# Issuing 29 small GpSimd loads of the front in quarter 3 instead of quarter 2, on one core

## The reference

```
sh1, sc1, gt1, sh2, sc2, gt2 = split(silu(c) @ w_ada + b_ada, 6)     # 9 conditioning rows, w_ada 2048 x 12288
h = rmsnorm(x, g_mix) * (1 + sc1) + sh1
qa, ka, va, qb, kb, vb, rb, ab = split(h @ w_in)                      # w_in 2048 x 4368
lg = log_sigmoid(ab @ w_gla_gate + b_gla_gate) / 16
oa = attention over a window, with learned sinks
     (prompt: own keys; sample: cache_swa_k, cache_swa_v and the new keys)
s_new, ob = gated linear attention(state_gla, qb, kb, vb, lg)
x = x + gt1 * (concat(oa, rmsnorm_head(ob, g_gla_norm) * silu(rb)) @ w_out)
h = rmsnorm(x, g_ffn) * (1 + sc2) + sh2
x = x + gt2 * top-2 of 32 experts(h)                                  # 3 x 4 MB of weights each, all 32 are read
y = rmsnorm(x, g_final)
```

## Time and profile before

| | |
|---|---|
| time, median of 3 runs | 1881.46 us (1879.25 to 1883.17) |
| the profiled execution: its own time | 1879.52 us |
| its span in the trace | 1877.9 us |
| TensorE busy | 1572.9 us, 84% |
| VectorE, ScalarE, GpSimd busy | 400.1, 201.2, 180.5 us |
| weights and large tensors, queue q1 | 562.29 MB, 73.8% of the engines' time |
| GpSimd's queue q0 | 41.68 MB, 7.3% |

### The profile page before, as it was taken

One profiled execution on the slowest core, in us unless ns is written; L12 is line 12 of the kernel. 1 busy time (PEld: TensorE's weight loads), 2 busy tenths in 40 slices (PEclk: granted clock), 3 DMA queues, 4 the chain that ended last, 5 costly groups with the idle time before them and its releaser, 6 DMA issues.

```text
span 1877.9 us, 21572 instructions
## 1 busy us (share of the span) xinstructions
PE 1572.9 (84%) x8837; PEld 812.9 (43%) x8837; DVE 400.1 (21%) x882; ACT 201.2 (11%) x505; POOL 180.5 (10%) x369
## 2 busy tenths in 40 slices
PE   6899999999999999958879888787877778888740
PEld 2355454444454444545445444444444344444320
DVE  2012222224232310452111111111111111111115
ACT  3001111111211100110000000000000000000003
POOL 1301000000101020030101001010101010101002
PEclk9999999999999999969889899999999998989985
DMA  9987777666623583199999999999999999999962
GB/s 365 336 291 289 280 280 290 245 257 230 224 68 101 179 247 118 68 332 397 426 426 427 427 427 428 426 423 426 427 426 424 425 421 420 417 426 426 426 246 96
DMA packets 101700, 610.94 MB, mean 325 GB/s; under 512 B 15950, under 2 KB 18110, under 8 KB 65418
## 3 DMA queue, kind: packets, MB, share of 16 engines
q1 hardware_dynamic: 84242, 562.29, 73.8%
q0 software_dynamic: 16592, 41.68, 7.3%
q10 hardware_dynamic: 816, 6.29, 0.8%
HBM read 603.03 MB, written 28.40 MB: 336 GB/s over the span
## 4 chain that ended last, share of the span: by engine, by line
PE 49%; DMA 43%; DVE 3%; issue 1%; ACT 1%; POOL 1%; SPq 0%; POOLq 0%; DVEq 0%; ACTq 0%
DMA ring<-in_w_expert_up 36%; PE bank L811 9%; PE bank L1111 7%; PE bank L807 7%; PE bank L1239 7%; DMA zbuf<-h_rows,cur 4%; PE bank L1260 3%; PE bank L765 3%; PE bank L1138 2%; PE bank L752 2%; DMA ring<-in_w_ada 2%; PE bank L731 1%; PE bank L756 1%; DMA ring<-in_w_in 1%; DVE ring L2122 1%
## 5 line engine op out<-in xcount | busy, mean ns | idle before, releaser
L1239 PE MATMUL bank<-ring,zbuf 128*64 128x256 f32 x4096 | 462.6, 382 | 81.0 <-DMA ring<-in_w_expert_up 72.7
L1239 PEld LDWEIGHTS bank<-ring,zbuf 128*64 128x64 f32 x4096 | 291.8, 137 | 259.7 <-DMA ring<-in_w_expert_up 94.9
L1260 PE MATMUL bank<-ring,hbuf 128*64 128x512 f32 x1024 | 270.5, 689 | 17.7 <-ACT hbuf L1550 17.7
L811 PE MATMUL bank<-ring,hbuf 128*128 128x512 f32 x384 | 174.2, 599 | 2.9 <-ACT xbuf L1343 2.6
L1260 PEld LDWEIGHTS bank<-ring,hbuf 128*64 128x64 f32 x1024 | 82.8, 158 | 185.7 <-issue 184.2
L807 PE MATMUL bank<-hbuf,ring 128*128 128x384 f32 x384 | 133.8, 495 | 1.2 <-ACT zbuf L1339 0.8
L1111 PE MATMUL bank<-ring,zbuf 128*128 128x512 f32 x288 | 128.7, 602 | 3.1 <-DVE ring L1858 1.9
L2027 DVE TENSOR_SCALAR hbuf<-hbuf 128x256 f32<-128x256 f32 x32 | 9.4, 294 | 520.2 <-ACT hbuf L1542 520.2
L811 PEld LDWEIGHTS bank<-ring,hbuf 128*128 128x128 f32 x384 | 70.2, 190 | 83.7 <-issue 82.7
L807 PEld LDWEIGHTS bank<-hbuf,ring 128*128 128x128 f32 x384 | 69.7, 190 | 52.5 <-issue 11.0
L631 POOL CAST cur<-stab 128x1 int32 (+1 forms) x32 | 5.7, 178 | 861.1 <-DVE zbuf L2035 861.1
(11 more groups left out here) (381 smaller groups left out, 1148.4 us busy)
## 6 DMA issues: line engine op xcount, KB each, us to landing
ring<-in_w_expert_gate SPq DMA_DIRECT2D x64, 2048.0 KB, 25.0
ring<-in_w_expert_down SPq DMA_DIRECT2D x64, 2048.0 KB, 23.3
ring<-in_w_expert_up SPq DMA_DIRECT2D x64, 2048.0 KB
ring<-in_w_ada SPq DMA_DIRECT2D x96, 1024.0 KB, 8.2
ring<-in_w_in SPq DMA_DIRECT2D x32, 1024.0 KB, 9.0
ring<-in_w_out SPq DMA_DIRECT2D x16, 1024.0 KB, 5.1
ring<-y_rows ACTq DMA_DIRECT2D x3, 2048.0 KB, 12.4
xbuf<-in_x_prompt SPq DMA_DIRECT2D x4, 1024.0 KB, 5.8
```

The lines of the kernel that those rows point to most:

```text
L811: last = mm(bank[t][:, :], hT[:, k, t * P:(t + 1) * P], w[:, kk_, :], start=(k == 0), stop=(k == KC - 1))
L1239: last = mm(bank[2 + u][64 * q:64 * q + 64, 256 * (j // 4):256 * (j // 4) + 256], xeT[u][:, k % 8, k // 8, :], w[:, kk_, 256 * q:256 * q + ...
L1260: last = mm(bank[5 + n][64 * q:64 * q + 64, :], hidT[u][:, k % 2, k // 2, :], unit(8 + k)[:, 1024 * q + QN * n:1024 * q + QN * n + QN], st ...
```

## The change

The wait of GpSimd at line 501 is raised from `modT_ps` 4 to 7, so that the 29 transfers are issued behind `columns(3, 0)` in place of `columns(1, 1)`. The order among them changes as well: the sinks, the gate's weight and bias and the head gain now come ahead of the second norm's gain and the bias rows. The transfers are the same 29 with the same sizes, and nothing else is changed.

```diff
-            pool.wait_ge(modT_ps, 4)
+            pool.wait_ge(modT_ps, 7)
             ck = A["cache_swa_k"][0].rearrange("b w j c -> w b j c")
             for u in range(2):
                 for j in range(SWA_KV):
                     g.dma_start(cache_k2[:, :, j, u, :], ck[:, :, j, :]).then_inc(cache_in, 16)
             g.dma_start(cache_v[:, :, :], A["cache_swa_v"][0].rearrange("b w j c -> w b (j c)")).then_inc(cache_in, 16)
+            pool.wait_ge(gate_zero, 1)
+            g.dma_start(sinkb[:, :], A["attn_sinks"].broadcast_to([P, SWA_H])).then_inc(small_in, 16)
+            for q in range(4):
+                g.dma_start(wgate[32 * q:32 * q + 16, :], A["w_gla_gate"][0]).then_inc(small_in, 16)
+            g.dma_start(wgate[16:17, :], A["b_gla_gate"]).then_inc(small_in, 16)
+            g.dma_start(gheadb[:, :], A["g_gla_norm"].broadcast_to([P, DV])).then_inc(small_in, 16)
+            sk = A["attn_sinks"].rearrange("a (j h u) -> u h a j", j=SWA_KV, u=2)
...
             bv = A["b_ada"][0].rearrange("(m g c) -> g m c", m=NMOD, g=4)
             gf = A["g_ffn_norm"].rearrange("a (g c) -> g a c", g=4)
...
-            pool.wait_ge(gate_zero, 1)
-            for q in range(4):
-                g.dma_start(wgate[32 * q:32 * q + 16, :], A["w_gla_gate"][0]).then_inc(small_in, 16)
...
             g.dma_start(slots_dram.rearrange("(p c) a -> p (c a)", p=P), empty[:, :]).then_inc(slots_init, 16)
```

More of the change, by code:

```diff
@@ L506, in _ @@
             g.dma_start(cache_v[:, :, :], A["cache_swa_v"][0].rearrange("b w j c -> w b (j c)")).then_inc(cache_in, 16)
+            pool.wait_ge(gate_zero, 1)
[5 more added lines that the diff above has]
+            sk = A["attn_sinks"].rearrange("a (j h u) -> u h a j", j=SWA_KV, u=2)
+            for u in range(2):
+                for h in range(4):
+                    r = 64 * u + 16 * h
+                    g.dma_start(sinks_s[r:r + 16, :], sk[u, h].broadcast_to([16, SWA_KV]),
+                                allow_slow_non_contiguous=True).then_inc(small_in, 16)
             bv = A["b_ada"][0].rearrange("(m g c) -> g m c", m=NMOD, g=4)
```

## The result

| | time, us, median (lowest to highest) | ratio to the kernel before, with its 95% interval |
|---|---|---|
| before | 1880.81 (1879.25 to 1883.17), 6 runs | |
| the change | 1865.97 (1862.98 to 1868.37), 6 runs | 0.9918 (0.9908 to 0.9928) |

The change makes the kernel faster by 0.8%, 14.8 us between the medians. The forecast was 1866.7 us. The profiled execution of the changed kernel took 1862.98 us, with a span of 1861.3.

The account below looks back on a forecast made before the run. TensorE bounds the front, then the expert weights' transfers do. Removing 14.15 us and adding 0 gave 1865.4 us profiled, 1867.3 us from the median and 1866.7 us from the mean, the forecast; range 1863 to 1875.

Parts of the forecast that it names:

- What bounds the kernel: Whole kernel: TensorE first, then the expert weights' transfers; TensorE's gain in the front should arrive at the end undiminished.
- The removed disturbance, 14.15 us: Quarter 2, between marks of line 741: 10.99 plus 3.16 us over undisturbed steps, 14.15 us, all taken as gain.
- Its two parts: Quarter 2: the 14.15 us are 7.72 us of two TensorE gaps and 6.43 us of low clock behind them.
- The second case: Collision moves with the loads, delaying quarter 3's last w_in pieces: gain 5.2 us, 1875.7 us, at worst 1879.0; chance 0.12.
- What is late next in quarter 2: Quarter 2 without the small loads: weights land in 7 to 8 us, so nothing is late and 14.15 us return.
- The third case: Quarter 2: the weights alone bound it, with 1 us to spare; gain 11.5 us, time 1869.4 us; chance 0.08.
- The new place costs nothing: Behind columns(3, 0): 8 to 9 us of loads fit empty engines, 4 us meet a burst with 12.6 us slack; cost 0.
- The loads' own use: After the new place: loads arrive before use, with slack of 16.3 us for cached values and 22 us for sinks.
- The fifth case: Line 833: cached keys come too late for TensorE, making the kernel slower; 38 us of delay would give 1888; chance 0.03.
- The rule that spoke against the change: DMA engines alternate between queues packet by packet, so moving the loads changes only whom they take time from; 45.7% against 59.1%.
- The fourth: Quarter 2: the gaps come from w_ada itself or are given back later; time stays at 1880.9 us; chance 0.03.

Follow-up runs that it names:

- e1: Kernel before with only the wait raised from 4 to 7, old order of the 29 loads kept; 1866.22 us, ratio 0.9914.
- e2: Changed kernel with the wait back at 4, so only the new order of the loads remains; 1878.88 us, ratio 0.9986.
- e3: Kernel before plus 24 unread products ahead of each of steps 4 and 5 of quarter 2; 1879.27 us, ratio 0.9987.
- e9: Kernel before plus 24 unread products ahead of step 4 and 16 ahead of step 5 of quarter 2; 1878.98 us, ratio 0.9993.
- e7: Changed kernel with the wait at 8, all 29 loads behind columns(3, 1); 1866.65 us, ratio 0.9927.
- e6: Changed kernel with the wait at 6, all 29 loads behind columns(2, 1), at the start of quarter 3; 1876.26 us, ratio 0.9982.
- e10: Changed kernel with the wait at 2, all 29 loads behind columns(0, 1), at the start of quarter 1; 1880.71 us, ratio 1.0005.

## Why the prediction was right

**What bounds the kernel.** Right. TensorE's gain in the front came out at the end. The stretch from 154 to 600 us takes 446.0 us in both, and what follows the last mark takes about as long in all thirteen traces.

**The removed disturbance, 14.15 us.** Right in size: 14.15 us between the same marks, 14.8 us between the medians, with an interval of 0.0072 to 0.0092 of 1880.81 us, 13.5 to 17.3 us. e1 and e2 show that it was the place of the loads.

**Its two parts.** Here the step failed: "The remaining 6.43 us are a low clock". The runs showed 1.4 to 3.2 us for the clock (e3 and e9), and 11 to 13 us for the lag of the transfers. In the kernel before, TensorE at low clock was running behind pieces that had not landed, so at least half of the slow work cost nothing. The forecast was not hurt, since it was taken from marks and not from the two parts, which go together; with the parts forecast one by one it would have been. The second case was hurt, where gaps were multiplied by 1.83: a lag of 11 to 13 us cost 14.15, 1.1 to 1.3 times its length.

**What is late next in quarter 2.** Nothing, as taken. The third case (the weights alone bound the quarter, 11.5 us) did not come: TensorE had work in 27.40 of 27.40 us. The 1 us of margin in 26.9 held. That q0's engine time, 12.5 us, is about the lag of the transfers (11 to 13 us) is what e3 and e9 add.

**The new place costs nothing.** Right, for partly other reasons. The last w_in pieces of quarter 3 landed in 8.5 and 9.4 us (9.0 and 9.8 before), not because sharing was harmless, but because the queues hardly shared: the small loads' packets came when the weights' were nearly through. And "The other 4 us ... meet the next burst" looked only at the first full piece of the burst. The pieces behind it were the tighter ones. The next w_in piece took 11.6 us, not 5.0, and 7.6 us were left; the one of the three w_ada pieces whose landing the trace tells took 16.0 us, not 9.2, and 7.3 us were left (142.0 against 149.36). The delay of these was 6.6 to 6.8 us, not 4. e7, with all of the loads 9 us later, shows that there is no step just behind the new place.

**The loads' own use.** Right, on the safe side. The cached values were in at 117.24 + 6.3 = 123.5 us, 22 us ahead of line 833, where 16.3 had been worked out from their slow landing in the old place. The fifth case did not come.

**The rule that spoke against the change.** The prediction read it from an average, 45.7% against 59.1%, over a window in which q0 was partly without work. In 75 to 92 us of the kernel before, where both queues have work all the time:

```profile
q0 software_dynamic: 871, 2.76, 62.7%
q1 hardware_dynamic: 881, 1.74, 41.3%
```

The numbers of packets are equal, and the shares are not: the packets of the small loads were the longer ones (3.2 KB in the mean against 2.0), and the small loads held three fifths of the engines. The Trainium skill (DMA: Bandwidth & Descriptors, Queues, rings and completion order) has the engines go round the queues packet by packet, and the trace agrees, with 871 packets against 881. In the burst behind the new place the counts are equal as well, 416 and 415, but there the weights' packets are the long ones (7.0 KB against 2.9) and the weights keep 70.7%. So the rule held in both places. It did not speak against the change, since the last weights of quarter 3 were nearly through when the loads' packets began, and since what it took from the burst met slack.

**The other cases.** The second (the collision moves along) is what e6 and e10 do, at 12 to 16 us: it was a question of 17 us of position. The range was given as taking in the milder part of this case, but its time, 1875.7 us, lies just outside 1863 to 1875. The fourth (the gaps are no work of q0) is refuted by e1, which changes nothing but the place.

## What to carry to other kernels

When DMA share is 1.0 and a ring of weights is used as fast as it is filled, a small load is not small: here it cost the bound engine about the engine time that its queue took (12.5 us of it, for a lag of 11 to 13 us). Find the stretch in which the engines are empty, because the ring is full or the weights have all been issued, and let the loads start there, even if that is only just ahead of their use. Then look for the tightest piece of the next burst, not its first, and find the first use of a piece in the code, not by the next line of the timeline that might be it. And price a stall from marks, quarter against quarter: the parts into which it seems to fall can overlap.

## What the runs showed of the hardware

- Two queues with work got the same number of packets through, 871 and 881 in 75 to 92 us before and 416 and 415 in 131 to 145 us of the change; the shares of the engines followed the packets' length, 62.7% to 41.3% for the small loads in the one and 29.9% to 70.7% in the other.
- The same load of cached values landed in 6.3 us where the engines became free and in 11.3 us where they were full. A landing time read in a full stretch says little about another.
- A stretch of low clock behind a gap costs less than its length says, if what comes in it is late anyway: 16.9 us at 0.61 cost some 1.4 to 3.2 us.
- The granted clock does not fall behind every gap of a given length. Behind the same gap of 1.85 us ahead of line 1111 it fell in the trace of before, for 3.4 us, and not in that of the change; behind a gap of 3.20 us at 44 us it fell in e1 and not in e6.
